# GpSimd updates three of the eight chunks at five norms, and products of ones stand in TensorE's waits

## The reference

```python
def swiglu(h, w_gu, w_down):
    g, u = jnp.split(h @ w_gu, 2, axis=-1)
    return (jax.nn.silu(g) * u) @ w_down
...
    for i in range(DEPTH):
        f = swiglu(rms_norm(h, ln_ffn1[i, 0]), ffn1_w_gu[i], ffn1_w_down[i])
        h = h + 0.5 * rms_norm(f, ln_ffn1[i, 1])
        hn = rms_norm(h, ln_mix[i, 0])
        ...
        h = h + rms_norm(m, ln_mix[i, 1])
        f = swiglu(rms_norm(h, ln_ffn2[i, 0]), ffn2_w_gu[i], ffn2_w_down[i])
        h = h + 0.5 * rms_norm(f, ln_ffn2[i, 1])
    return h[:, N_META:]
...
# second block, for each of its two layers
        mod = cond @ ada_w[l] + ada_b[l]
        shift, scale, gate = jnp.split(mod, 3, axis=-1)
        h = rms_norm_2(x, norm_g[l]) * (1.0 + scale[:, None, :]) + shift[:, None, :]
        ...
        x = x + gate[:, None, :] * y
```

## Time and profile before

| | before |
|---|---|
| median of 3 runs | 1360.51 us (1358.34 to 1362.44) |
| profiled execution | 1358.39 us |
| its span | 1356.6 us |
| TensorE busy | 97% of the span |
| VectorE, ScalarE, GpSimd busy | 67%, 60%, 8% |
| mean granted clock of TensorE | 0.986 of full speed |

### The profile page before, as it was taken

The page is one execution under the profiler, slowest core; times in us unless marked ns, Lnnn a source line. Parts: engine busy times, 40 slices in busy tenths (PEclk is TensorE's granted clock), DMA queues, the critical chain, the costliest instruction groups (busy, mean ns, idle before and its releaser), DMA issues.

```text
span 1356.6 us, 27964 instructions
## 1 busy us (share of the span) xinstructions
PE 1320.9 (97%) x10456; PEld 1290.8 (95%) x10456; DVE 908.2 (67%) x1487; ACT 811.7 (60%) x1575; POOL 104.1 (8%) x118
## 2 busy tenths in 40 slices
PE   7999999999999999999999999899999899989998
PEld 7999999998999999999999898799999899989998
DVE  7877536976877645877645777578864575565665
ACT  7766644446776645776644565677774453546674
POOL 2000011012000002000002211110000100000000
PEclk9999998999999999999998999999999999989999
DMA  7777653554777743777742543367775253345341
GB/s 253 237 219 229 224 178 137 176 174 135 237 229 230 235 153 118 237 229 224 240 162 78 161 132 98 125 202 241 240 260 177 89 166 114 101 151 187 125 125 63
DMA packets 64613, 240.54 MB, mean 177 GB/s; under 512 B 7905, under 2 KB 9361, under 8 KB 64529
## 3 DMA queue, kind: packets, MB, share of 16 engines
q1 hardware_dynamic: 63312, 238.77, 54.9%
q0 software_dynamic: 1216, 0.60, 0.2%
HBM read 237.70 MB, written 1.05 MB: 176 GB/s over the span
## 4 chain that ended last, share of the span: by engine, by line
PE 89%; DVE 4%; ACT 4%; DMA 1%; issue 1%; POOL 1%; SPq 0%; ACTq 0%; DVEq 0%; POOLq 0%
PE bank L1848 25%; PE bank L1850 25%; PE bank L1849 25%; PE bank L1899 2%; DVE w_lo L1127 2%; PE bank L1900 1%; PE bank L1892 1%; ACT w_hi L613 1%; PE bank L2222 1%; ACT ada_raw L699 1%; PE bank L2206 1%; PE bank L2205 1%; PE bank L2207 1%; DVE h L1189 1%; ACT x_hl L654 1%
## 5 line engine op out<-in xcount | busy, mean ns | idle before, releaser
L1127 DVE TENSOR_TENSOR w_lo<-raw,w_hi 128x1024 fp32r<-128x1024 f32 (+2 forms) x376 | 488.6, 1304 | 260.8 <-ACT w_hi L613 260.8
L1848 PE MATMUL bank<-x_hl,w_hi 128*128 128x272 f32 (+1 forms) x2008 | 580.9, 289 | 5.0 <-DVE x_hl L1195 4.6
L1850 PE MATMUL bank<-x_hl,w_lo 128*128 128x272 f32 (+1 forms) x2008 | 575.9, 287 | 0.0
L1849 PE MATMUL bank<-x_hl,w_hi 128*128 128x272 f32 (+1 forms) x2008 | 573.6, 286 | 0.0
L613 ACT ACTIVATE w_hi<-raw 128x1024 fp32r<-128x1024 f32 (+2 forms) x376 | 409.9, 1096 | 148.1 <-PE bank L1850 130.8
L1848 PEld LDWEIGHTS bank<-x_hl,w_hi 128*128 128x128 f32 x2008 | 379.5, 189 | 6.5 <-ACT x_hl L654 4.6
L1849 PEld LDWEIGHTS bank<-x_hl,w_hi 128*128 128x128 f32 x2008 | 382.0, 190 | 0.4
L1850 PEld LDWEIGHTS bank<-x_hl,w_lo 128*128 128x128 f32 x2008 | 378.9, 189 | 0.0
L1848 PE MATMUL bank<-a_hi,w_hi 128*128 128x272 f32 (+1 forms) x960 | 277.2, 289 | 2.4 <-DVE a_lo L1249 1.5
L1850 PE MATMUL bank<-a_hi,w_lo 128*128 128x272 f32 (+1 forms) x960 | 273.5, 285 | 0.0
L1849 PE MATMUL bank<-a_lo,w_hi 128*128 128x272 f32 (+1 forms) x960 | 273.0, 284 | 0.0
(11 more groups left out here) (277 smaller groups left out, 1273.3 us busy)
## 6 DMA issues: line engine op xcount, KB each, us to landing
raw<-w SPq DMA_DIRECT2D x312, 512.0 KB, 4.3
raw<-w SPq DMA_DIRECT2D x64, 704.0 KB, 4.4
ada_raw<-ada_w SPq DMA_DIRECT2D x48, 512.0 KB, 3.6
h<-x_in SPq DMA_DIRECT2D x2, 544.0 KB, 5.8
work<-bands SPq DMA_DIRECT2D x1, 544.0 KB, 6.5
arena<-arena POOLq DMA_DIRECT2D x32, 17.0 KB, 3.5
out<-h SPq DMA_DIRECT2D x1, 512.0 KB, 2.9
out<-h SPq DMA_DIRECT2D x4, 128.0 KB, 2.8
```

Source lines behind the costliest of these rows:

```text
L1127: ve.tensor_tensor(w_lo[:, s, cols], raw[:, s, cols], w_hi[:, s, cols].bitcast(F32), ALU.subtract).then_inc(w_lo_ready, 1)
L1848: te.matmul(dst, w_hi[:, s, a:a + P], rhs_hi, start=first, stop=False)
L1849: te.matmul(dst, w_hi[:, s, a:a + P], rhs_lo, start=False, stop=False)
L1850: return te.matmul(dst, w_lo[:, s, a:a + P], rhs_hi, start=False, stop=last)
```

## The change

Nothing is computed otherwise; steps move between engines, and products are added whose results nobody reads.

- At the five norms GpSimd does the steps t and h of chunks 5, 6 and 7 (`updates`), queued ahead of the tree. VectorE does the other five chunks singly. The hi steps of 5, 6 and 7 wait for GpSimd. TensorE and ScalarE take the chunks in the order 0 1 2 5 3 6 4 7, and VectorE's split of a weight (line 1127) now stands ahead of lo7, no longer behind it.
- At `res3` VectorE does chunks 2 and 3 singly.
- The modulation products have 64 equal columns where they had one, and the result is read with a step.
- `keep_clock` issues products of a 128x128 matrix of ones with itself: nine at the start, one ahead of and ten behind the last sum of squares at cout and aout, eight ahead of the first quad of ein and ten ahead of that of oin.
- The token sum of `second_quad` moves from behind the first unit to behind the second chunk of the second unit.

```diff
+        ADA_COLS, ADA_STEP = 64, 32
...
-        def together(c):
-            return slice(c, c + 1) if c < 2 else slice(c, c + 2)
-        def h_step(c):
-            return f"h{c}" if c < 2 else f"h{c - c % 2}"
+        ENTER_ORDER = (0, 1, 2, 5, 3, 6, 4, 7)
+        ENTER_ACT = ["hi0", "hi1", "sq0", "hi2", "sq1", "hi5", "sq2", "hi3", "sq5", "hi6", "sq3", "hi4", "sq6", "hi7", "sq4", "sq7"]
+        ENTER_VEC = ["t0", "h0", "t1", "h1", "lo0", "t2", "h2", "lo1", "lo2", "t3", "h3", "lo5", "t4", "h4", "lo3", "lo6", "lo4",
+                     "lo7"]
+        ENTER_POOL = ["t5", "h5", "t6", "h6", "t7", "h7"]
...
                     if step[:2] == "hi":
-                        sc.wait_ge(vec.sem, vec.at(phase, h_step(c)))
+                        if c >= 5:
+                            sc.wait_ge(pool.sem, pool.at(phase + "u", f"h{c}"))
+                        else:
+                            sc.wait_ge(vec.sem, vec.at(phase, f"h{c}"))
...
-                split_lo(stage, 0, 3)
+                    if step == "lo4":
+                        split_lo(stage, 0, 3)
...
-            for c in (0, 1, 2):
+            for c in range(5):
                 normed("res3", c, SEQ)
                 added("res3", c, slice(META, T), SEQ)
...
+            def updates(res, phase):
+                ts, n = toks(phase), width(phase)
+                gp.wait_ge(act.sem, act.at(res, "r"))
+                for c in (5, 6, 7):
+                    gp.tensor_tensor(f[:, c, 0:n], f[:, c, 0:n], r_t[:, 0:n], ALU.mult).then_inc(pool.step(phase + "u", f"t{c}"), 1)
+                    gp.wait_ge(pool.sem, pool.at(phase + "u", f"t{c}"))
+                    gp.tensor_tensor(h[:, c, ts], f[:, c, 0:n], h[:, c, ts], ALU.add).then_inc(pool.step(phase + "u", f"h{c}"), 1)
...
-                    last = te.matmul(ADA[:, i:i + 1], ada_sum[:, i, :], ones[:, 0:1], start=True, stop=True)
+                    last = te.matmul(ADA[:, i * ADA_STEP:i * ADA_STEP + ADA_COLS], ada_sum[:, i, :], ones[:, 0:ADA_COLS], start=True, stop=True)
...
+            def keep_clock(n, spare):
+                for _ in range(n):
+                    te.matmul(spare[:, 0:P], ones[:, :], ones[:, :], start=True, stop=True)
...
+                keep_clock(1, bank[7])
                 res_last("resc", act.at("cout", "sq3", 1))
+                keep_clock(10, bank[7])
```

More of the change, by code:

```diff
@@ L925, in _ @@
                 else:
-                    pre_square("pree", c, (vec.sem, vec.at("res3", h_step(c))))
+                    pre_square("pree", c, (vec.sem, vec.at("res3", f"h{c}")))
             pre_rms("pree")
@@ L1500, in _ @@
             ve.wait_ge(act.sem, act.at("res3", "r"))
-            for c in (0, 1, 2):
+            for c in range(5):
                 normed("res3", c, SEQ)
                 added("res3", c, slice(META, T), SEQ)
-            ve.tensor_tensor(f[:, 4, 0:SEQ], f[:, 4, 0:SEQ], r_t[:, 0:SEQ], ALU.mult).then_inc(vec.step("res3", "t4"), 1)
-            own("res3", "t4")
-            ve.tensor_tensor(h[:, 4, META:T], f[:, 4, 0:SEQ], h[:, 4, META:T], ALU.add).then_inc(vec.step("res3", "h4"), 1)
             add_mod(3)
@@ L1808, in _ @@
             ffn_sums(0, None)
+            updates("res0", "prec")
             tree("prec")
             out1("cout", ("res0", "ss"))
+            updates("resc", "pre1")
             tree("pre1")
             ffn_sums(1, ("resc", "ss"))
+            updates("res1", "pre2")
             tree("pre2")
             ffn_sums(2, ("res1", "ss"))
+            updates("res2", "prea")
             tree("prea")
@@ L1827, in _ @@
             out1("aout", ("res2", "ss"))
+            updates("resa", "pre3")
             tree("pre3")
@@ L1876, in project, with unit @@
                 quads(stage, quad)
-            def unit(stage, dst, s, n):
+            def unit(stage, dst, s, n, between=None):
                 for k in range(DC):
+                    if between and k == 2:
+                        between()
                     last = product(dst[:, 0:n], s, k, x_hi[:, k, 0:n], x_lo[:, k, 0:n], k == 0, k == DC - 1)
@@ L1887, in first_quad @@
                 te.wait_ge(w_lo_ready, SLOTS * q + 3)
+                order = range(DC) if phase in ("pree", "preo") else ENTER_ORDER
+                begin, end = order[0], order[DC - 1]
                 def lower(k):
@@ L1891, in lower @@
                     for s in range(3):
-                        last = te.matmul(dsts[s][:, 0:n], w_hi[:, s, k * P:(k + 1) * P], x_lo[:, k, 0:n], start=False, stop=k == DC - 1)
-                        if k == DC - 1:
+                        last = te.matmul(dsts[s][:, 0:n], w_hi[:, s, k * P:(k + 1) * P], x_lo[:, k, 0:n], start=False, stop=k == end)
+                        if k == end:
                             last.then_inc(unit_done, 1)
-                for k in range(DC):
+                for j, k in enumerate(order):
                     te.wait_ge(act.sem, act.at(phase, f"hi{k}"))
                     for s in range(3):
-                        te.matmul(dsts[s][:, 0:n], w_hi[:, s, k * P:(k + 1) * P], x_hi[:, k, 0:n], start=k == 0, stop=False)
+                        te.matmul(dsts[s][:, 0:n], w_hi[:, s, k * P:(k + 1) * P], x_hi[:, k, 0:n], start=k == begin, stop=False)
                         te.matmul(dsts[s][:, 0:n], w_lo[:, s, k * P:(k + 1) * P], x_hi[:, k, 0:n], start=False, stop=False)
-                    if k:
-                        lower(k - 1)
-                lower(DC - 1)
+                    if j:
+                        lower(order[j - 1])
+                lower(end)
                 te.wait_ge(w_lo_ready, SLOTS * q + 4)
@@ L1909, in second_quad, with token_sum @@
                 q = FIRST_QUAD[stage] + 1
+                def token_sum():
+                    te.wait_ge(pool.sem, pool.at(phase, "tr2"))
+                    te.matmul(bank[2][:, 0:n], ones[:, :], sq8[:, 0, 0:n], start=True, stop=True).then_inc(pe.step(phase, "ss"), 1)
                 for s in range(SLOTS):
@@ L1915, in second_quad @@
                         te.wait_ge(*free)
-                    unit(stage, bank[s], s, n)
-                    if s == 0:
-                        te.wait_ge(pool.sem, pool.at(phase, "tr2"))
-                        te.matmul(bank[2][:, 0:n], ones[:, :], sq8[:, 0, 0:n], start=True, stop=True).then_inc(pe.step(phase, "ss"), 1)
+                    unit(stage, bank[s], s, n, token_sum if s == 1 else None)
             def later_quads(stage, n, free):
```

21 lines of the change are left out of this document (10 added, 11 removed).

## The result

The changed kernel takes 1374.01 us (median of five runs, 1373.06 to 1374.18), the kernel before 1360.51 (1358.34 to 1362.44). The ratio is 1.0096, with a 95% interval from 1.0084 to 1.0107: slower by 13.5 us. The profiled execution took 1373.06 us, with a span of 1370.8 us, 14.2 more than before.

What follows compares the result with a forecast made beforehand. TensorE's own work, waits and half clock were taken as the bound. Norms + 7.5 less 3.45, new clock falls + 3.0, prea + 2.2, res3 + 0.3, preo - 0.4 made + 9.2 us; it named 1368 us, range 1364 to 1374.

Steps and rivals of the forecast that it cites:

- preo at its bound: At preo, the upper bound of + 2 us, where the net effect of the ten products of ones was put at - 0.4.
- a fourth unit at 13.9 to 15.5 us: At the five norms, the unit that ends the norm starts that long after r_t, against 12.2 to 13.5 before.
- GpSimd holds VectorE up: At the entering norms, both engines alternate, 0.92 us per pair; hi2 ends 1.9 us later (1.8 at 256 columns).
- Rivals 1 and 2: Norms: 1, GpSimd doesn't hold VectorE up, 1349 to 1351, chance 0.22; 2, lo isn't held up, 1360 to 1362, 0.24.
- lo7, now behind the weight split, ends near 13.3, when TensorE would reach it at 13.7: At the norms, VectorE's last lo step is done before TensorE needs it, so the 57 products stay the longer side.
- - 3.45 and + 3.0: Clock kept up at prec, pre1, pre2, pre3 gives back 3.45 us; new falls in about two norms cost 1.5 each.
- 4.8 us was put down to half clock at the norms: At the five norms, what half clock cost in the kernel before, the most that keeping the clock could give.
- The products are free: Wider modulation products and products of ones cost nothing at full clock, at 0.107 us an instruction, upper bound 0.23.
- prea, + 2.2: Ahead of the first scores, ScalarE's last square and so GpSimd's tree come later, and the scores 2.2 us later.
- Token sum, 0: In second_quad, the sum moves behind six more products, 0.75 us, but its cover grows, so it costs nothing.
- res3 + 0.3: At res3, VectorE does chunks 2 and 3 singly; h4 ends 0.3 us later and the last squares wait for it.
- preo - 0.4: At preo, ones at half clock delay 1.8 us; clock back after 3.4 us gives 2.2; bounds - 2.3 and + 2.

Runs made afterwards that it cites:

- late_share: The kernel of lo7_first, with GpSimd starting its six operations only when VectorE has done h2; 1361.66 us, 1.0002 of the kernel before.
- lo7_first: The changed kernel with lo7 again ahead of the weight split; 1368.68 us, 1.0061 of the kernel before.
- clock_only: The kernel before with all added products (64-column modulation, products of ones) and nothing moved between engines; 1356.98 us, ratio 0.9976.
- tree_quarters: The changed kernel with the first addition of GpSimd's tree cut into four of 128x272; 1367.86 us, 1.0053 of the kernel before.
- share_only: The changed kernel with one-column modulation products and no products of ones; 1376.11 us, 1.0120 of the kernel before.
- sum_back: The changed kernel with the token sum again behind the first unit; 1372.51 us, 1.0086 of the kernel before.
- scores_ones: The kernel of clock_only with 20 products of ones ahead of the first scores; 1354.73 us, 0.9952 of the kernel before.
- vec_all: The changed kernel without GpSimd's share: VectorE does all chunks singly, in order, lo7 ahead of the weight split; 1357.97 us, ratio 0.9985.

## Why the prediction was nearly right

It said slower, 1368 us, from 1364 to 1374; it is 1374.0, at the upper edge. Its mechanism is shown, its sum was 5 us too small (+ 9.2 where the span grew by 14.2), and one of its steps was wrong. That the range just held the result is luck: its top stood for a clock that falls at all four norms and for preo at its bound, and neither came; the missing 5 us came from lo7. The sign that it named for itself, a fourth unit at 13.9 to 15.5 us, failed at four norms of five (15.75 to 15.87). There is also a slip in its last step: + 9.2 on the median of 1360.5 gives 1369.7, not 1368.

- **GpSimd holds VectorE up: right.** h takes 0.88 us beside GpSimd (0.92 was said for 272 columns, 0.87 read at 256), hi2 ends at 6.56 us (6.55). What no row of before showed, lo is held up as well: 0.99 us. Rivals 1 and 2 fall with this. late_share shows that it is the hold-up ahead of h2 that counts. By itself this part was sized well: at pre1, with the clock up in both, the fourth unit stands 1.7 us later in lo7_first than in clock_only, where 1.9 was said.
- **"lo7, now behind the weight split, ends near 13.3, when TensorE would reach it at 13.7": wrong.** This is the step that failed. lo7's start was nearly right (12.48 us after r_t), but the tree starts at 12.34, and the alternation that the prediction had just read in the earlier trace rows holds there too, only that the other instruction has 1088 columns. lo7 ends at 15.24. lo7 takes 2.76 us where 0.50 was put. The prediction counted the tree only for prea and for the token sum, and never asked what ran on VectorE when it began. lo7_first and tree_quarters, two unlike ways of taking the collision away, give back 5.3 and 6.1 us by the medians.
- **Clock: half right.** It did fall again, and later than before: at prec and pre2, two of the four norms as was said, and at prea besides. But the terms - 3.45 and + 3.0 were worth nothing here up to the fourth unit, since lo7 covered them (share_only). The value itself was a little high: 4.8 us was put down to half clock at the norms, the fourth units of clock_only get 3.6. The 57 products from hi2 on last 7.4 us there at full clock (527.57 to 534.99 us at pre2), 0.13 each, where 7.1 were put, so less of the time before was due to the clock.
- **The products are free: right.** clock_only holds them all and is faster. They last 0.11 us an instruction, at 64 as at 128 columns.
- **prea, + 2.2: right in sign, other in way.** The scores came 3.1 us later. It wasn't the tree that decided: started ahead of lo7, it ended at 17.3 us after r_t (16.9 before). ScalarE's copies of q and k wait behind weight splits that wait for the first quad, and so for lo7; the swap was issued at 20.1 (17.7 before).
- **Token sum, 0: wrong by 0.76 us at one norm.** The prediction asked whether the sum has its input in time, and not who waits for its output. In cin TensorE does.
- **res3 + 0.3 and preo - 0.4:** + 0.25 and - 0.65, near by number. At preo the ten products took 3.67 us and the first product with hi0 started 2.20 us after r_t, 1.27 before: 0.9 us late, 1.8 was put. The clock was back after 3.4 us, as said, but the reason given (TensorE busy all the time) has a row against it: at prea in the earlier trace rows it was busy for all of 6.83 us and at half clock as long. Whether the clock falls at preo at all differs between traces with the same work there: without a fall (tree_quarters, late_share, sum_back) the stretch from r_t on is 0.9 us shorter still.
- **The start, not in the sum:** its - 0.56 can't be put down to the change. Over all traces r_t of prec lies between 212.3 and 214.8 us, and in two the clock falls once near 14 us.

Summed: the norms were said to cost 9.25 us with prea (4.05 + 3.0 + 2.2) and cost 15.15.

The Trainium skill says in "SBUF — State Buffer" (Who interferes with whom) that who issues first keeps the shared port for the whole instruction; it says so of VectorE's two-port modes. By the 2.76 and 1.02 us above, much the same is true of an operation with two inputs in SBUF. The prediction had read the rule so (the engine that comes second blocks wholly) and used it for lo0, but not for lo7 and the tree. The tree's first addition took 2.60 us and began 0.14 us ahead: an estimate from these is 2.46 us of waiting and 0.50 of work, 2.96 us, where 2.76 was measured.

Two more falls of the clock stood in the trace of before, behind the first scores (756.4 to 759.8 us) and at res3 (1070.5 to 1073.9 us), and the prediction missed them. In clock_only the one at the scores comes sooner and lasts twice as long, 6.8 us. With the longer wait there it is part of why clock_only won less than expected: 20 products of ones in that wait took 1.5 us off the stretch (scores_ones). The 4.8 us that were really 3.6 are another part.

## What to carry to other kernels

In this kernel work moved to GpSimd wasn't taken off VectorE, since both read two tiles from SBUF: count such work as turns that the two take. What an operation loses is about the rest of the instruction that came first, so ask of every long one of either engine which short, urgent one may come just behind it, and cut the long one or put the urgent one ahead. When a step of an engine comes sooner, look for what it now overlaps: in clock_only it was the tree, and the next idle stretch cost the clock. And follow a gain to the next point where engines meet: 6.0 us at the fourth units of vec_all had become a loss of 0.5 by the next r_t's.

## What was not expected of the hardware

- A 272-column operation took 2.76 us because it started 0.14 us behind a 1088-column one of GpSimd; behind a 272-column one, 1.02 us. What one engine is spared the other pays: the tree takes 4.97 us where lo7 waits for it, 7.39 us where a weight split is ahead.
- With the share for GpSimd the clock didn't fall at the same norms in kernels that are alike up to hi2: at prec, pre2 and prea in the changed kernel, at pre2, prea and pre3 in tree_quarters, at prec, pre1, prea and pre3 in sum_back. Each is one execution; over its five executions the changed kernel's mean clock went from 0.990 to 0.995, so it isn't fixed by the program alone. What decides it was not settled.
- Where a fall lies counts more than that it happens: one of 3.4 us that began 2.3 to 2.4 us after r_t (prea in lo7_first, pre2 in tree_quarters) was over before hi2 and left the fourth unit where full clock puts it.
